# The opening of a 1-core two-block network kernel: first weights ahead of the third modulation piece, x's roots on GpSimd, x turned around the first piece

## The reference, cut to what matters

```python
sc  = silu(c)                                    # c: 1 x 1024
mod = (sc @ ada_w[0] + ada_b[0]).reshape(9, 1024)  # shift, scale, gate, three times
h   = rmsnorm(x, g[0]) * (1.0 + mod[1]) + mod[0]   # x: 256 x 1024
gate, up = split(h @ ffn_w_in[0, 0])             # 1024 x 5632
x   = x + 0.5 * (1.0 + mod[2]) * rmsnorm((silu(gate) * up) @ ffn_w_out[0, 0], g[1])
```

## Time and profile before

| | |
|---|---|
| median of three runs | 1582.57 us (1580.81 to 1582.78) |
| profiled execution | 1577.79 us |
| its span, first to last instruction | 1576.0 us |
| TensorE busy | 1535.4 us, 97% of the span |
| VectorE, ScalarE, GpSimd busy | 1211.4, 881.0, 81.6 us |
| granted TensorE clock, mean | 0.994 |

### The profile page before, as it was taken

One profiled execution on the slowest core, in us unless ns is written; L12 is line 12 of the kernel. 1 busy time (PEld: TensorE's weight loads), 2 busy tenths in 40 slices (PEclk: granted clock), 3 DMA queues, 4 the chain that ended last, 5 costly groups with the idle time before them and its releaser, 6 DMA issues.

```text
span 1576.0 us, 19285 instructions
## 1 busy us (share of the span) xinstructions
PE 1535.4 (97%) x7477; PEld 1246.0 (79%) x7477; DVE 1211.4 (77%) x1752; ACT 881.0 (56%) x1341; POOL 81.6 (5%) x135
## 2 busy tenths in 40 slices
PE   7999999999999999999999999999999999999998
PEld 3888886888887888867878888777788888787876
DVE  2898878988867888664476654769888789988896
ACT  3544445544447444377474544655567477777774
POOL 1110100000002000010011000000001000000000
PEclk9999999999999999999999999899999999999999
DMA  9999856988857988333277554445323469989893
GB/s 346 375 378 350 292 200 203 336 303 301 300 175 268 325 286 307 122 108 108 80 269 200 187 165 137 154 142 187 113 101 118 173 236 358 341 309 337 325 338 133
DMA packets 196338, 373.76 MB, mean 237 GB/s; under 512 B 8986, under 2 KB 102608, under 8 KB 196240
## 3 DMA queue, kind: packets, MB, share of 16 engines
q1 hardware_dynamic: 176688, 301.08, 55.6%
q0 software_dynamic: 18864, 69.76, 12.8%
q10 hardware_dynamic: 688, 1.62, 0.3%
HBM read 371.38 MB, written 1.05 MB: 236 GB/s over the span
## 4 chain that ended last, share of the span: by engine, by line
PE 88%; ACT 5%; DVE 5%; DMA 1%; issue 1%; SPq 0%; POOL 0%; DVEq 0%; ACTq 0%
PE banks L524 25%; PE banks L526 24%; PE banks L525 24%; PE banks L1609 1%; PE banks L1084 1%; DVE ul L460 1%; ACT arena L762 1%; ACT uh L449 1%; PE banks L635 1%; PE banks L1582 1%; PE banks L2139 1%; PE banks L1596 1%; DMA raw<-in_ffn_w_in 1%; PE banks L2741 1%; PE banks L936 1%
## 5 line engine op out<-in xcount | busy, mean ns | idle before, releaser
L449 ACT ACTIVATE uh<-raw 128x1024 fp32r<-128x1024 f32 (+2 forms) x548 | 568.9, 1049 | 393.5 <-PE banks L526 389.5
L460 DVE TENSOR_TENSOR ul<-raw,uh 128x1024 fp32r<-128x1024 f32 (+2 forms) x548 | 657.1, 1209 | 149.9 <-ACT uh L449 142.0
L524 PE MATMUL banks<-uh,hh 128*128 128x512 f32 (+2 forms) x1296 | 514.9, 397 | 10.4 <-DVE hl L1029 6.5
L526 PE MATMUL banks<-uh,hl 128*128 128x512 f32 (+2 forms) x1296 | 503.1, 388 | 0.0
L525 PE MATMUL banks<-ul,hh 128*128 128x512 f32 (+2 forms) x1296 | 502.0, 387 | 0.0
L524 PEld LDWEIGHTS banks<-uh,hh 128*128 128x128 f32 x1296 | 244.5, 189 | 65.8 <-DVE hl L1029 10.1
L526 PEld LDWEIGHTS banks<-uh,hl 128*128 128x128 f32 x1296 | 244.3, 189 | 50.7
L525 PEld LDWEIGHTS banks<-ul,hh 128*128 128x128 f32 x1296 | 244.9, 189 | 46.1 <-issue 0.5
L524 PE MATMUL banks<-uh,bh 128*128 128x512 f32 x512 | 207.1, 404 | 1.0 <-DVE bl L2938 0.9
L526 PE MATMUL banks<-uh,bl 128*128 128x512 f32 x512 | 199.7, 390 | 0.0
L525 PE MATMUL banks<-ul,bh 128*128 128x512 f32 x512 | 199.4, 389 | 0.0
(11 more groups left out here) (356 smaller groups left out, 1280.3 us busy)
## 6 DMA issues: line engine op xcount, KB each, us to landing
raw<-in_ffn_w_in SPq DMA_DIRECT2D x176, 512.0 KB, 6.7
raw<-in_w_up SPq DMA_DIRECT2D x64, 1024.0 KB, 7.1
arena<-in_ada_w POOLq DMA_DIRECT2D x60, 1024.0 KB, 6.2
raw<-in_ffn_w_out SPq DMA_DIRECT2D x44, 1024.0 KB, 5.5
raw<-in_w_down SPq DMA_DIRECT2D x32, 1024.0 KB, 7.0
raw<-in_w_in SPq DMA_DIRECT2D x22, 1024.0 KB, 4.9
raw<-in_ada_w SPq DMA_DIRECT2D x12, 1024.0 KB, 10.8
raw<-in_w_mem_kv SPq DMA_DIRECT2D x4, 1024.0 KB, 5.1
```

Source lines behind the costliest of these rows:

```text
L449: act.e.activation(uh[r][:, 0:w], raw[m % NRAW][:, h * w:(h + 1) * w], AF.Copy).then_inc(act_done, ta.put("hi", u))
L460: dve.e.tensor_tensor(ul[r][:, 0:w], raw[m % NRAW][:, h * w:(h + 1) * w], uh[r][:, 0:w].bitcast(F32), ALU.subtract).then_inc(dve_done, tv. ...
L524: pe.e.matmul(o, a, wh, start=k + j == s0, stop=False)
L526: mm = pe.e.matmul(o, b, wh, start=False, stop=k + j == s1)
```

## The change

It does six things. (1) In the plan, the first chunk of feed-forward weights moves from place 6 to place 4, ahead of piece 2, whose chunks become 5 and 6; chunks 7 to 9 and all later ones keep their places. (2) The bias products are a function of their own, and those of pieces 0 and 1 are put ahead of everything, those of pieces 2 and 3 ahead of the first feed-forward unit. (3) TensorE turns groups 0 and 1 of x before the products of piece 0 and groups 2 and 3 after them; totals 0 and 1 come after the products of piece 1. (4) The products of piece 2 move from before the first feed-forward unit to behind it; those of piece 3 move from before the second unit's first tile to behind it. (5) The reciprocal roots of x are made by GpSimd, for each row tile an addition and a power; ScalarE's root, its two table loads and VectorE's four steps go. (6) ScalarE and VectorE skip and copy the pieces in the new order.

```diff
-    for a in ADA_FIRST[:3]:
+    for a in ADA_FIRST[:2]:
         ada(*a)
-    ffn(0, 0, ADA_FIRST[3:])
+    ffn(0, 0, ADA_FIRST[2:])
...
-            ada_parts_pe(pe, first[0], 2)
+            ada_bias_pe(pe, first[0], 2)
+            ada_bias_pe(pe, first[1], 3)
             pe.wait_ge(loaded("small"), 16 * len(SMALL))
             pe.e.transpose(PB[6][:, 128:128 + NSMALL], stk2[0:NSMALL, :], ident[0:NSMALL, 0:NSMALL]).then_inc(
                 pe_done, tp.put("smallT"))
             pe.frees(6, dve_done, tv, "cc")
             turn((0, 1))
+            ada_products_pe(pe, first[0], 2)
+            turn((2, 3))
+            ada_products_pe(pe, first[1], 3)
             total(0)
-            ada_parts_pe(pe, first[1], 3)
             total(1)
-            turn((2, 3))
-            ada_parts_pe(pe, first[2], 2)
+            ada_bias_pe(pe, first[2], 2)
+            ada_bias_pe(pe, first[3], 3)
 
             got = [take_unit(pe, up_key(0, 0)(0)) for _ in range(2)]
             for t in range(T):
                 mm = first_parts(*got[0], 0, t)
             mm.then_inc(pe_done, tp.put("used", got[0][0]))
-            ada_parts_pe(pe, first[3], 3)
+            ada_products_pe(pe, first[2], 2)
             first_parts(*got[1], 2, 0)
+            ada_products_pe(pe, first[3], 3)
             total(2)
             total(3)
...
-            diag_act(act, 0, lambda t: act.wait_ge(loaded(f"x{t}"), 16), junk=x_junk)
-            act.wait_ge(loaded("sum4"), 16)
-            silu_table_act(act)
+            for t in range(T):
+                act.wait_ge(loaded(f"x{t}"), 16)
+                squares_act(act, st[:, 4 + t:5 + t], x[:, t, :], "xsq", 0, t, junk=x_junk, scale=D ** -0.5)
...
             piece(0)
             piece(1)
-            ada_skip(act, ADA_FIRST[2])
             split_high(act, act.unit_at)
...
-            ada_copy_act(act, ADA_FIRST[2], 2, START_BUFS[2])
+            piece(2)
             piece(3)
...
-            diag_dve(dve, 0)
+            for t in range(T):
+                dve.wait_ge(pool_done, tg("xr", 0, t))
+                dve.e.tensor_scalar(dgx[t], ident[:, :], st[:, 6 + t:7 + t], None, ALU.mult).then_inc(
+                    dve_done, tv.put("dg", 0, t))
...
-            pool.wait_ge(act_done, ta("xsq", 0, 1))
+            for t in range(T):
+                r = st[:, 6 + t:7 + t]
+                pool.wait_ge(act_done, ta("xsq", 0, t))
+                pool.wait_ge(pool_done, tg.n)
+                pool.e.tensor_scalar(r, st[:, 4 + t:5 + t], EPS, None, ALU.add).then_inc(pool_done, tg.put())
+                pool.wait_ge(pool_done, tg.n)
+                pool.e.tensor_tensor(r, r, minus_half, ALU.pow).then_inc(pool_done, tg.put("xr", 0, t))
```

More of the change, by code:

```diff
@@ L596, in idle, with ada_bias_pe @@
                 yield w
[L599 to L602, removed]
+        def ada_bias_pe(pe, a, b):
+            r = a[0] * 18 + a[1]
             pe.wait_ge(loaded("ident"), 16)
@@ L607, in ada_parts_pe, with ada_products_pe @@
                         start=True, stop=False)
+        def ada_products_pe(pe, a, b):
+            got = [take_raw(pe, ("ada",) + a) for _ in range(2)]
             pe.wait_ge(act_done, ta("sc"))
@@ L618, in ada_parts_pe @@
             pe.frees(b, act_done, ta, "ada_c", a)
+        def ada_parts_pe(pe, a, b):
+            ada_bias_pe(pe, a, b)
+            ada_products_pe(pe, a, b)
         def ada_skip(eng, a):
@@ L1332, in start_dve @@
             dve.e.memset(ones[:, :], 1.0).then_inc(dve_done, tv.put("ones"))
-            for n in range(3):
+            for n in range(2):
                 ada_skip(dve, ADA_FIRST[n])
@@ L1340, in start_dve @@
                 take_unit(dve, up_key(0, 0)(0))
-            ada_skip(dve, ADA_FIRST[3])
+            for n in (2, 3):
+                ada_skip(dve, ADA_FIRST[n])
             for n in (2, 3):
```

## The result

| | before | after |
|---|---|---|
| median, 22 runs each | 1580.96 us (1575.55 to 1583.98) | 1578.14 us (1572.08 to 1579.48) |
| ratio after to before, 95% interval | | 0.9984 (0.9976 to 0.9991) |
| profiled execution | 1577.79 us | 1578.11 us |
| its span | 1576.0 us | 1576.3 us |
| TensorE's first feed-forward product | 30.07 us | 26.08 us |

0.16% of 1581 us is a gain of 2.5 us, between 1.4 and 3.8; I had forecast 3.1. But the two profiled executions show a gain of only 1.3 us in the row that I said is worth the whole change, and their spans none. Both need an explanation.

The account below looks back on a forecast made before the run. TensorE bounds from the second weight half on; the opening gains 5.2 us, less 1.2 for the wait, 0.8 for bare copy and order, 0.1 for chunk 9: 3.1, so 1582.57 - 3.1 = 1579.5 us; range 1576.8 to 1582.7.

Parts of the forecast that it names:

- The bound: From the second weight half's first product (42.27 us) TensorE bounds; opening gains before it reach the end us for us.
- Rival E: No gain: transfers, at 1.06 share, fall behind in the first blocks and give 3.1 us back, 1582.6; chance 0.05.
- rival B: Opening's chunks land earlier, chunk 8 up to 0.9 us; gain 4.0 us, 1578.6; chance 0.18.
- Roots, small loads, biases, first turn: Opening: diagonals ready about 9.9, biases done 9.9, small loads gate the turn at 10.6, low clock to 14.2.
- Piece 0, "all behind it at the high one": Behind the first turn the clock is high: piece 0 to 16.1, second turn to 18.1, piece 1 to 20.0.
- rival C: Clock rises late, only in the second turn: gain 0.8 to 2.4 us, about 1581.0; chance 0.20.
- First unit, "12 products of 0.23": First feed-forward unit: from first product at 24.9, 12 products at 0.23 us pitch, to 27.7.
- rival D: Slower: clock stays low until the feed-forward products; 5.5 us slower, 1588.1; chance 0.07.
- The wait for chunk 8: Middle of piece 3: TensorE, ready at 32.1, waits for the landing at 33.2; 1.2 us lost.

Follow-up runs that it names:

- e5: Changed kernel with the chunk order of before (first weights as chunk 6, piece 2 ahead of first unit, piece 3 ahead of second); ratio 1.0018 to kernel before.
- e6: Changed kernel with x's roots back on ScalarE and VectorE, and the two table loads; ratio 0.9991 to the kernel before.
- e9: Against e7: bias products of piece 2 in place of the second filler, behind the second turn; ratio 0.9962 to the kernel before.
- e7: Changed kernel with second turn behind totals 0 and 1, eight fillers behind piece 0, eight behind that turn, biases 2 and 3 back with their pieces; ratio 0.9984.
- e11: e9 unchanged, run again for more runs and a second profile; ratio 0.9977 to the kernel before.
- e12: e11 with x's roots back on ScalarE and VectorE; ratio 0.9987 to the kernel before.
- e3: Changed kernel with the second turn of x put back behind totals 0 and 1; ratio 0.9994 to the kernel before.
- e2: Changed kernel with twelve filler products on TensorE behind the bias products, ahead of the first feed-forward product; ratio 0.9993 to the kernel before.
- e1: Changed kernel once more, no edit, for a second profile; ratio 0.9982 to the kernel before.

## Why the prediction was right, and where its steps failed

The time is right, and by luck; the path is not. I had said that the prediction is wrong if the second half starts off 39.1 by over 1 us: it starts at 40.93, 41.88 and 41.07. And a range from 1576.8 to 1582.7 holds even 1580.96, no gain at all.

**The bound.** Right. TensorE is the bound from the second half on, and the shift of that row is carried unchanged to 200 us and beyond. Rival E fell: the transfers gave nothing back. So did rival B: chunk 8 landed at 33.0, not up to 0.9 us ahead of 33.2.

**Roots, small loads, biases, first turn.** Right to 0.2 us: diagonals at 10.1 (9.9), small loads the gate, with TensorE waiting 0.5 us for the last of them, turn at 10.67 (10.6), 3.78 us long at the low level (3.66).

**Piece 0, "all behind it at the high one".** Wrong by 1.0 us. The clock rose not at the turn's end, 14.4, but inside piece 0, which took 2.87 us; in three profiles of the changed kernel it took 2.84 to 3.07, in e5, e6 and e9 1.92. This is the small form of rival C, and with total 0, 0.9 us on TensorE between piece 1 and total 1, for which my sum had left only 0.7, it makes the first product late: 26.08 for 24.9.

**First unit, "12 products of 0.23".** This is the step that failed. I had taken the clock to hold once it was up, and had counted biases in idle time at nothing. They took no time on the path, but they were not free: the order puts piece 1, two totals and two bias pairs in a row, 5.6 us of narrow products, where before a turn of wide ones stood between total 1 and piece 2. The clock fell, and the twelve products took 4.5 us instead of 2.8. It is rival D's mechanism in another place and at a smaller price: I had priced a clock that stays low from the start, with 0.07, and not one that rises and falls again. The gain of 1.3 us in the row lies in the span that rival C names, 0.8 to 2.4, though not for its reason alone. With wide products between the narrow ones (e7, e9, e11, e12) the twelve products started 0.23 us apart, as summed.

**The wait for chunk 8.** 1.2 us in my sum, none in the profile. Not because the chunk came early (33.0 for 33.2) but because TensorE came late: of the 2.9 us lost by then (34.02 for 31.1), 1.2 were hidden in this wait. The rest, 1.7 us, is the gap between 39.1 and 40.93, with 0.1 of small change. With the clock held the wait appeared, and the row came to 39.65 and 39.40.

**Numbers.** The forecast of 3.1 us was that of an opening the change does not have. Its own rows bring 1.3, 0.6 and 1.1 us, measured from chunk 0; the runs say 2.5 (1.4 to 3.8), 2.8 (0.6 to 4.9) and 1.1 (-0.3 to 2.5) in three comparisons. The difference between the rows and the first two of these lies in the low stretches further on, which I can't attribute: whether the shifted opening makes them rarer or whether it is chance stays open. The forecast time was 1579.5, the measured one 1578.14: the kernel before ran 1.6 us faster beside the changed one (1580.96) than in the three runs that I started from (1582.57), and the gain fell short by 0.6. The time fell into the range because both errors were smaller than the range.

**When the clock rises.** In this case's rows the first rise comes between 14 us (e9, whose piece 0 at 13.97 takes 1.92) and the end of the first turn at about 18.5 (before). The Trainium skill (TensorE: Matmul & The Clock Gate, "What's actually happening") has activity release the half rate, and the trace agrees as far as the rise came while TensorE worked: 16 products took 3.78 us at 10.67 and 2.05 at 17.19. I had taken from this only that the clock rises, and not that it can fall again while TensorE works.

## What to carry to other kernels

When work is reordered ahead of a wait, look at what TensorE does there and at the granted clock behind it, and not only at whether it is busy: products 32 columns wide, of one column or of few rows count as busy in the profile, and here the clock fell behind a row of them, with and without a wait. It held in all four profiles in which wide products (a turn that was needed anyway, and a filler behind piece 0) stood between the narrow ones; the late turn without that filler (e3) didn't hold it, and a filler behind the narrow products (e2) ran at half speed and made things worse. And price an opening by one row that all later work follows, against a landmark such as the first landing, when executions of the same kernel differ by more than the change.

## What the runs showed of the hardware

The granted clock fell to 0.50 at 24.0 us (e1) and 24.2 (e2) though TensorE had shown no wait since 11. The same eight products took 1.99 or 3.24 us at 260 us in two kernels that do not differ there; the mean granted clock of a run, 0.991 to 0.997 for one and the same kernel, goes with 5 us and more of its time. The windows show a clock of 1.00 ahead of its first rise, where durations say half: 16 products of a turn took 3.78 us at 10.67 and 2.05 at 17.19, both under 1.00. So at the opening the durations, and not the clock's column, tell the level.
